# The first mixer rewritten in an fp32 transformer kernel: local-attention steps and GLA work set between projection tiles

## Time and profile before

| | us |
|---|---|
| median of 3 runs (1872.35 to 1878.27) | 1877.52 |
| profiled execution, its own time | 1876.8 |
| its span, first to last instruction | 1875.0 |
| PE busy in the span | 1820.0 (97%), granted clock 0.974 in the mean |
| VectorE, ScalarE, GpSimd busy | 939.5, 746.1, 716.8 |
| first mixer, start to the last product of W_out | 297.2 |
| the MLP of the first block and all behind it | 1577.8 |

### The profile page before, as it was taken

How to read it: one execution, slowest core, us unless ns; L and a number is a source line. 1 busy time by engine, 2 the same in 40 slices (tenths; PEclk the granted TensorE clock), 3 DMA queues, 4 the chain that set the end, 5 groups by cost and what they waited for, 6 DMA issues and landing times.

```text
span 1875.0 us, 24546 instructions
## 1 busy us (share of the span) xinstructions
PE 1820.0 (97%) x8248; PEld 1449.3 (77%) x8248; DVE 939.5 (50%) x1627; ACT 746.1 (40%) x1224; POOL 716.8 (38%) x311
## 2 busy tenths in 40 slices
PE   7988899999999999999999999999999999999997
PEld 4666678888888877877888888887777778888886
DVE  4844344555531145555625161657777773526164
ACT  4444235555542244333423232445555442323243
POOL 2322024444444432333444444444444344444443
PEclk9999679999999999998999999999999999999999
DMA  5221012333333432221333332332232132323222
GB/s 157 80 67 36 11 45 90 90 100 101 91 99 101 131 97 74 84 71 56 92 98 100 90 101 90 100 129 86 97 107 77 61 96 90 101 91 100 94 96 89
DMA packets 48053, 167.42 MB, mean 89 GB/s; under 512 B 5155, under 2 KB 6451, under 8 KB 47830
## 3 DMA queue, kind: packets, MB, share of 16 engines
q1 hardware_dynamic: 47894, 166.43, 28.3%
q10 hardware_dynamic: 96, 0.15, 0.1%
HBM read 164.31 MB, written 2.24 MB: 89 GB/s over the span
## 4 chain that ended last, share of the span: by engine, by line
PE 89%; DVE 6%; issue 3%; ACT 2%; DMA 0%; DVEq 0%; SPq 0%; ACTq 0%
PE bank L432 15%; PE bank L433 14%; PE bank L438 14%; PE bank L740 12%; PE bank L674 4%; PE bank L679 4%; PE bank L675 4%; PE bank L718 2%; PE bank L717 2%; PE bank L723 2%; PE bank L975 1%; PE bank L1004 1%; DVE tmp L2177 1%; PE bank L641 1%; PE bank L821 1%
## 5 line engine op out<-in xcount | busy, mean ns | idle before, releaser
L368 POOL TENSOR_TENSOR w_lo<-stage,w_hi 128x1024 fp32r<-128x1024 f32 x284 | 685.8, 2415 | 1066.8 <-ACT w_hi L1108 620.3
L1108 ACT ACTIVATE w_hi<-stage 128x1024 fp32r<-128x1024 f32 x284 | 299.6, 1055 | 393.5 <-PE bank L433 295.3
L432 PE MATMUL bank<-xn_hi,w_hi 128*128 128x512 f32 x688 | 277.8, 404 | 11.6 <-ACT w_hi L1108 9.6
L433 PE MATMUL bank<-xn_lo,w_hi 128*128 128x512 f32 x688 | 271.9, 395 | 0.0
L432 PE MATMUL bank<-arena,w_hi 128*128 128x512 f32 x608 | 237.8, 391 | 3.5 <-DVE x L1573 1.7
L433 PE MATMUL bank<-arena,w_hi 128*128 128x512 f32 x608 | 236.7, 389 | 0.0
L2177 DVE TENSOR_TENSOR tmp<-tmp,rstd 128x512 f32<-128x512 f32 x64 | 149.4, 2334 | 115.4 <-ACT tmp L1524 115.4
L438 PE MATMUL bank<-xn_hi,w_lo 128*128 128x512 f32 x688 | 171.5, 390 | 0.0
L432 PEld LDWEIGHTS bank<-xn_hi,w_hi 128*128 128x128 f32 x688 | 131.4, 191 | 48.5 <-ACT w_hi L1108 9.6
L438 PE MATMUL bank<-arena,w_lo 128*128 128x512 f32 x608 | 160.5, 389 | 0.0
L433 PEld LDWEIGHTS bank<-xn_lo,w_hi 128*128 128x128 f32 x688 | 131.7, 191 | 28.6 <-issue 1.9
(11 more groups left out here) (275 smaller groups left out, 2663.1 us busy)
## 6 DMA issues: line engine op xcount, KB each, us to landing
stage<-weights SPq DMA_DIRECT2D x284, 512.0 KB, 3.6
bias<-table SPq DMA_DIRECT2D x11, 896.0 KB, 5.4
out<-z SPq DMA_DIRECT2D x8, 256.0 KB, 2.7
x<-x_in SPq DMA_DIRECT2D x1, 1024.0 KB, 9.2
bias<-swa_table SPq DMA_DIRECT2D x4, 256.0 KB, 3.7
con<-consts SPq DMA_DIRECT2D x1, 640.0 KB, 11.9
bias<-table SPq DMA_DIRECT2D x5, 128.0 KB, 3.7
par<-params SPq DMA_DIRECT2D x1, 515.0 KB, 4.1
```

What stands on the lines that cost most here:

```text
L368: nc.gpsimd.tensor_tensor(w_lo[:, p_], stage[:, p_], w_hi[:, p_].bitcast(F32), ALU.subtract).then_inc(lo_ready, 1)
L432: pe.matmul(G[p_][:], w_hi[:, p_, k], hi[:, k], start=(first and k == ks[0]), stop=False)
L433: mm = pe.matmul(G[p_][:], w_hi[:, p_, k], lo[:, k], start=False, stop=False)
L1108: act.activation(w_hi[:, p_], stage[:, p_], ACT.Copy).then_inc(hi_ready, 1)
```

## The change

- **Start.** The DMAs are cut smaller: the first eight columns of `par`, then x and the first two weight tiles in halves. Tiles 0 and 1 are multiplied together, k by k, as x comes; squares and their sum come after the splits of x; memsets of `v_tok` and `acc` are gone.
- **One local-attention step per tile.** For tiles t = 4..17 `step(t - 4)` stands in the middle of the tile (after 12 of its 24 products): the transposes of block i-1, the values of block i-2, the scores of block i. Steps 14 to 17 stand between W_out's tiles. The dense tiles come in a new order, `IN_ORDER`.
- **Values.** Not padded; each of the two heads writes its 64 partitions of `OB`. Both heads' transposes go to one bank and are copied by one ACT instruction.
- **q/k scales per token.** The mean squares are 4 products of 2 columns (`swn_sums`), the inverse root is found on 128x8 numbers, and 8 products with the identity spread it (`swn_spread`) into a bank from which DVE scales in one instruction. The 512-column square root and reciprocal are gone.
- **GLA between tiles.** Scores, states, outputs and mean squares of head pair j = 0 stand before tiles 10 to 13, of j = 1 at tiles 12, 15 and 16. The two heads of a pair alternate. States of a whole pair are written to two banks at once, and DVE chains them after (7 instructions of 128x128 for 28 of 64x128). silu is made of Exp and Ln, so no table is loaded.
- **W_out in K halves.** `out_part` (used so far by the third block) multiplies k = 0..3 (GLA's heads) for all eight outputs, then k = 4..7 (local attention) for all eight. DVE adds 16 times, not 8.
- **Low parts in quarters**, for all 284 tiles: POOL makes `w_lo` in four instructions of 128x256.

```diff
-                nc.gpsimd.tensor_tensor(w_lo[:, p_], stage[:, p_], w_hi[:, p_].bitcast(F32),
-                                        ALU.subtract).then_inc(lo_ready, 1)
+                for k in range(0, KD, KD // 4):
+                    ks = slice(k, k + KD // 4)
+                    ins = nc.gpsimd.tensor_tensor(w_lo[:, p_, ks], stage[:, p_, ks], w_hi[:, p_, ks].bitcast(F32), ALU.subtract)
+                ins.then_inc(lo_ready, 1)
...
+            def value(i):
...
+                for j in range(b - a):
+                    for h in range(2):
+                        r = slice(64 * h, 64 * h + 64)
+                        mm = pe.matmul(OB[r, n * P:(n + 1) * P], swa_v[:, a + j, r], swa_pT[:, n % 2, 2 * h + j],
+                                       start=(j == 0), stop=(j == b - a - 1))
                 mm.then_inc(swa.pv_done, 1)
...
+            def step(i):
+
+                if 0 <= i - 1 < 4 * NQ:
+                    turn(i - 1)
+                if 0 <= i - 2 < 4 * NQ:
+                    value(i - 2)
+                if 0 <= i < 4 * NQ:
+                    score(i)
...
+                for t in range(NQ):
+                    mm = pe.matmul(MB[:, 2 * t:2 * t + 2], tmp[:, i % 2, t * P:(t + 1) * P], ccol("mean_64")[:, 0::64],
+                                   start=True, stop=True)
+                mm.then_inc(swn_ss, 1)
...
+            def states(j):
...
+                for c in range(NCH - 1):
+                    r = slice(64 * (c % 2), 64 * (c % 2) + 64)
+                    for h in range(2):
+                        d = slice(64 * h, 64 * h + 64)
+                        mm = pe.matmul(SC[c % 2][d, c // 2 * P:(c // 2 + 1) * P], kd_tok[j][r, c // 2, d],
+                                       gv_tok[r, 2 * j + h, c // 2], start=True, stop=True)
+                mm.then_inc(state_in, 1)
...
+                elif t == 10:
+                    gla_scores(0)
+                elif t == 11:
+                    swn_spread(3)
+                    states(0)
+                elif t == 12:
+                    outputs(0)
+                    gla_scores(1)
+                elif t == 13:
+                    mean_squares(0)
+                    token_major(5)
+                elif t == 14:
+                    token_major(6)
+                elif t == 15:
+                    swn_spread(4)
+                    states(1)
+                elif t == 16:
+                    mean_squares(1)
...
+            for t in range(2, N_IN):
+                early(t)
+                dense(T_IN, t, 0, 12)
+                middle(t)
+                if t == 15:
+                    dense(T_IN, t, 12, 20)
+                    outputs(1)
+                    dense(T_IN, t, 20, 24)
+                else:
+                    dense(T_IN, t, 12, 24)
...
+            pe.wait_ge(gla_lo, 3)
+            out_tile(0, 0, [0, 1, 2])
+            out_tile(1, 0, [0, 1, 2])
+            step(14)
+            pe.wait_ge(gla_lo, GH)
+            out_tile(0, 0, [3])
+            out_tile(1, 0, [3])
+            out_tile(2, 0)
+            step(15)
...
+            def sigmoid(i):
+
+                in_done(Z_GR + i)
+                link("act", act, act.activation(gla_sig[i], z[:, Z_GR + i], ACT.Exp, scale=-1.0))
+                link("act", act, act.activation(gla_sig[i], gla_sig[i], ACT.Ln, bias=1.0))
+                act.activation(gla_sig[i], gla_sig[i], ACT.Exp, scale=-1.0).then_inc(sig_done, 1)
```

More of the change, by code:

```diff
@@ L668, in up_tile @@
+            pe.wait_ge(swa_lo, 4)
+            out_tile(0, 1, [7])
+            out_tile(1, 1, [7])
+            for d in range(2, KD):
+                out_tile(d, 1)
             def up_tile(m, p_, bank, first=False):
@@ new lines, in _ @@
+            sigmoid(3)
+            gla_high(2)
+            gla_high(3)
+            copy(13)
+            split(T_OUT + 2)
+            exps(14)
+            copy(14)
+            split(T_OUT + 3)
+            exps(15)
+            split(T_OUT + 4)
+            copy(15)
+            split(T_OUT + 5)
+            pair_high(3)
+            for d in range(KD):
+                if d % 2:
+                    split(T_OUT + 6 + d // 2)
+                act.wait_ge(evac[d % 2], T_OUT // 2 + WO_HALVES + d // 2 + 1)
+                act.activation(xn_hi[:, d], x[:, d], ACT.Copy, scale=pcol("ffn_norm", d, d + 1)).then_inc(xh_ready, 1)
+                act.activation(tmp[:, d % 2], x[:, d], ACT.Square).then_inc(sq_ready, 1)
@@ L1753, in _ @@
+            project(N_IN - 1)
+            gla_low(2)
+            scale(13)
+            gating(3)
+            gla_low(3)
+            maxima(14)
+            add_half(T_OUT, 0, 0)
+            add_half(T_OUT, 1, 0)
+            scale(14)
+            add_half(T_OUT, 2, 0)
+            maxima(15)
+            add_half(T_OUT, 3, 0)
+            scale(15)
+            add_half(T_OUT, 4, 0)
             dve.wait_ge(lam_exp, 1)
```

1090 lines of the change are left out of this document (595 added, 495 removed).

## The result

The changed kernel takes 1806.5 us (1805.8 to 1807.4, four runs), the one before beside it 1877.0 (1872.4 to 1878.3, four runs): ratio 0.963, 95% interval 0.961 to 0.965, 70.4 us less. I had forecast 54.8 less. The profiled execution has a span of 1804.3 us against 1875.0.

The account below looks back on a forecast made before the run. PE's path through the first mixer (297.2 us: plain fp32, waits, low clock) was to become 36.5 + 125.1 + 56.4 + 16.7 + 9.2 = 243.9; 1876.8 - 53.3 - 1.5 = 1822 us, own range 1810 to 1834, wide range 1802 to 1850.

Parts of the forecast that it names:

- Start, 36.5: First mixer to the end of tile 2: 36.5 us instead of 41.7, bounds 35 to 39.
- Plain fp32, 56.4: Plain fp32 products among the first mixer's dense tiles: 56.4 us together, bounds 50, and 68 if some don't pair.
- (a): New wait at tile 4: first scores wait for key and query scaled behind DVE's list, 3 us (0 to 5).
- (b): New wait ahead of W_out: PE waits for `gla_low(2)` behind queued DVE and ACT work, 8 us (4 to 11).
- (c): New wait for the mean squares at tile 16, as `outputs(1)` ends four products before: 0.7 us.
- Clock, 9.2: Low clock in the first mixer: 1.7 us behind tile 4's wait, 2.5 behind W_out's, 5 for fp32 blocks; together 9.2.
- Low parts in quarters, 1.5: Half of PE's 3.18 us wait at 839.05 goes, 1.5 us; all else is cover, 0.
- 1: Rival: clock stays low in the mixed stretch, tiles 10 to 17, 22 us over the allowance: 1844 us; chance 0.12.
- 2: Rival: VectorE's and ScalarE's in-order queues become the bound, 1.5 us a tile, 21 us: 1843 us; chance 0.14.
- rival 3: Quarters free more: shorter wait at 839.05 keeps the clock, saving some 8 us; with low-end new waits 1809; chance 0.13.
- 4: Rival: low parts come late, POOL over its period if a quarter exceeds 1.36 us; 2080 us at 1.6; chance 0.02.
- 5: Rival: little gained; start gains nothing, nothing pairs, waits and clock at top of bounds: 1862 us; chance 0.05.

Follow-up runs that it names:

- experiment 1: The changed kernel with each low part in one GpSimd instruction again instead of quarters: 1830.4 us, ratio to the kernel before 0.977.
- experiments 5: The changed kernel with tile 17 read before head 2's gating, head 2's high part before the last sigmoid, tile 18's local-attention step before W_out: 1803.6 us.
- 7: The changed kernel with the last pair's scaling ahead of the group row, and the mixer's end reordered so W_out's ready heads come first: 1794.5 us.
- experiment 6: The changed kernel with VectorE scaling the last pair's probabilities before, not after, its wait for the group weights' row (dilated attention's end): 1798.7 us.

## Why the prediction was right, and where not

The total came out 15.6 us under the forecast: the quarters gave 22 us more than I had allowed, and the other edits some 7 us less. The wide range, 1802 to 1850, held; the forecast's own, 1810 to 1834, missed. That the miss was no larger is partly luck, since the two errors have opposite signs: with whole low parts the MLP begins at 248 us (experiment 1), later than the 244 of my sum. Two of my signs failed with it, the MLP's first product at 240 to 250 us (238.6) and a stretch of 1576 or 1577 us behind it (1565.6).

The mixer's mechanism was right, though only the order of the heads and the quarters have runs of their own. By the two traces the 58.5 us are: the start 3.0; behind tile 2 PE idle 10.1 us instead of 25.4, so 15.3; and, as an estimate from the mean clocks (230.1 us busy at 0.86, 190.0 at 0.98), 28 us of low clock. The last 12 are fewer products, and products beside each other.

- **Start, 36.5.** Measured 38.65. Within my bounds (35 to 39). The start is clean at a clock of 1.00, but this rests on the quarters: with whole low parts there is a 2.0 us wait for x's low part and a clock of 0.93 to 0.96 up to 60 us.
- **Dense products, 125.1.** Not measured apart; kept at that here. Where other work stands on both sides, twelve products take 2.86 us instead of 2.72 (108.22 to 111.08), 0.3 more a tile, which falls to the next line.
- **Plain fp32, 56.4, and hand-overs, 5.** 238.7 less 38.65, 125.1, the waits behind tile 2 (10.0) and the clock (2.3) leaves 62.6, against 61.4. The single prices were not all right: values don't pair (0.15 each in either order), states cost 0.07 and not 0.13, outputs 4.5 for a pair and not 4.0, the mean squares 0.85 each and not 1.0.
- **New waits, 11.7 without the hand-overs.** (a) 1.0 for 3: the bound 0 to 5 held. (b) 6.75 for 8: right in kind and size; experiments 5 and 7 show that it is queueing. (c) none. Others, 2.2.
- **Clock, 9.2.** Mis-sized. Only the loss behind (b) came, 11 products at 0.43 instead of 0.23, 2.3 us. I took 5 us for fp32 blocks between dense tiles; they ran at 1.00 throughout. My reason, that GLA's blocks had run at 0.50, did not carry over, since the outputs now go in turn.
- **Low parts in quarters, 1.5.** The step that failed. I searched for the one place where PE waited behind a long VectorE instruction, and set all else to zero, "cover". But several waits of under 1 us do that too (behind the mixer the sum of all waits fell from 9.3 to 4.3 us), and the old mixer, which I left out, gains 6.6 us by itself. That error is there in the kernel before. A smaller one is that I priced the quarters only there: the step's chain, 3.35 us, I had read where GpSimd held nothing up (the addition L1622 at 161 ns); beside whole low parts the same addition takes 1359. Measured: 16 to 17 us before, 24 in the new kernel.

The rivals. 1: its premise, that this kind of work lowers the clock without a wait, is true of heads one after the other, and the change's order avoids it. 2: no; from 60 to 180 us PE waits for nothing. 3 came nearest, 1809: its mechanism is half there. The wait of 3.18 us went to 1.98, but the clock fell all the same, and only experiment 6 took the 8 us that rival 3 named. 4: a quarter costs 0.85 us and not 1.36; eighths come near to it. 5: no.

Open: 4 of the 12.2 us behind the mixer are by difference; the start, the new order of steps, the scales per token and W_out in halves have no run of their own, so how the 46 us without the quarters fall to them is not shown; what lowered the clock among the states of the kernel before; and what exactly the clock follows, since waits of 1.81 us kept it in one place and 1.56 with 0.42 didn't in another.

## What to carry to other kernels

Where GpSimd streams SBUF beside VectorE, cut its instructions until a piece is about as long as VectorE's own; price it in the kernel that it goes into, since each VectorE instruction with two SBUF inputs, however narrow, that moves onto TensorE's path beside GpSimd raises it. Order plain fp32 products so that those that use different parts of the array alternate: that halves some of them and kept the clock up here, while the other order lowered it with TensorE never idle. And fill the wait in front of an accumulation with whichever of its inputs are ready: two waits of together 2 us cost 7.9.

## What was new about the hardware

- 8 products of 128 columns and 14 of 64, fp32, one head after the other: the granted clock falls from 1.00 to 0.50 within the block, without any wait, and in eight rounds of it stays there for some 100 us; in turn it stays at 1.00 for the 37 us that eight rounds last, but in turn doesn't bring it back from 0.50 in 17.6 us.
- State products on a quarter of the array, of which rows and columns alternate, take 0.07 us each (14 in 1.02) against 0.15 one head after the other.
- A VectorE addition of two columns to two columns took 1359 ns in the mean of 16 beside GpSimd's 1024-column instructions and 161 where these did not stand in its way.
- GpSimd's `tensor_tensor` in 128, 256, 512 and 1024 columns takes 522, 852, 1380 and 2416 ns in the mean beside VectorE's work, so a further piece costs 0.25 to 0.34 us, an estimate from these four ((8 x 522 - 2416) / 7 and 2 x 1380 - 2416).
